# A third staging buffer and biased exponentials in the head stage of a two-block transformer kernel

## The chip, the cores and the metric

The kernel runs on one core of one Trainium2 chip. A core has TensorE (matmuls; PE in the rows, and PEld for its weight loads), VectorE (DVE), ScalarE (ACT), GpSimd (POOL) and SyncE (SP), each with an instruction queue of its own that is worked off in order, and DMA engines. The metric is the time of one execution on the device in microseconds. It covers two different transformer blocks of two layers each over 272 and 256 tokens. Every weight is read from HBM once, everything is computed in float32 precision.

## The reference

Block 1 is a mixer with three branches (retention, hgrn2, differential attention) and a convolutional feed-forward; block 2 has four branches, one of them a gated linear attention of the same form as hgrn2. The change is in how the decay of hgrn2 is applied, of which this is the core:

```python
def hgrn2(q, f_logit, inp, gate, lb, valid):
    log_f = logaddexp(log(max(lbh, LB_FLOOR)), log1p(-lbh) + log_sigmoid(f_logit))
    k = (1.0 - lbh) * sigmoid(-f_logit)
    def step(state, xs):
        qc, kc, vc, lfc = xs
        cb = cumsum(lfc, axis=1)
        dec = where(causal, exp(cb[:, :, None] - cb[:, None, :]), 0.0)
        a = einsum('bqhd,bkhd,bqkhd->bhqk', qc, kc, dec)
        o = einsum('bhqk,bkhe->bqhe', a, vc) + einsum('bqhd,bhde->bqhe', qc * exp(cb), state)
        c_end = cb[:, -1]
        state = exp(c_end)[..., None] * state + einsum('bkhd,bkhe->bhde', kc * exp(c_end[:, None] - cb), vc)
        return state, o
```

There are 8 heads of 128 features, and chunks of 128 tokens (128, 128 and 16).

## The kernel before

**Weights.** All weights come as slabs of eight 128x128 blocks through a ring of six slots. SyncE loads a slab when TensorE has released its slot (slab_used). ScalarE rounds it to ring_hi (L879), VectorE (L1318, in some stretches GpSimd, L2017) subtracts to ring_lo, and only then does TensorE use it. A product is three matmuls a block (hi x hi, lo x hi, hi x lo; L456), so a projection of a 128-feature tile is 24 matmuls and one slab.

**The order.** Each engine's program is written out by hand, in a fixed order; engines wait for each other with counted semaphores (Signal, Banks). PSUM has eight banks that all products take in turn. The head stage is the loop over the eight hgrn2 heads in block 1. TensorE does, for head h: the level products (masked block products at block sizes 64 to 1, "lv"), the products between chunks ("cross"), three projections out of TILES_FILL, the values times the weights, two more projections and the sum of squares. TILES_FILL holds the projections of the other branches, three rotated tiles (rq, rk, dq, dk) and two value tiles (rv, dv) for each head. Behind every projection the tile before it is turned (turn): a rotated tile is multiplied with a rotation matrix, a value tile is transposed (L533).

**Staging.** Before a tile can be turned, ScalarE copies it from PSUM to a buffer of XS (stage; the copy is followed by the drain L941 that signals it). XS has two buffers, so the copy of tile i waits for tile i-2: for a value tile until TensorE has transposed it, for a rotated tile until VectorE has taken it (settle, L1448 to L1453).

**Head h on VectorE:** hg_weights(h) masks and adds the level products (L1368 on); hg_differences(h+1) writes the exponents (L1397 to L1401 and L1352) into Z; then normalise(h-1), and a sequence of slabs and settled tiles; after the first settled tile hg_factors(h+1) multiplies the exponentials with the keys (L1360, L1410 to L1413) and signals z, without which TensorE can't begin the level products of head h+1. ScalarE's exp_levels(h+1) lies between the two, behind the copy of the second tile and ahead of that of the third. Z[:, 3] and Z[:, 8] hold the factors between chunks: the first chunk's keys carried to its end, the second chunk's queries from its start, the first chunk's keys carried to the end of the second (Z[:, 8, 0:P], the product of Z[:, 3, 0:P] and e1, the decay over the whole second chunk), the second chunk's keys carried to its end, and the 16 last queries. HC is the running sum of -log f in each chunk (L1656, eight scans). Block 2 has the same in one piece for its gated linear attention (L1937 to L1942, L1254).

## Time and profile before

| | |
|---|---|
| median of 3 runs | 2497.81 us (2497.37 to 2498.92) |
| the profiled execution | 2496.82 us, span 2495.0 us |
| granted TensorE clock, mean | 0.982 |
| TensorE busy | 2354.8 us, 94% |
| VectorE busy | 1807.5 us, 72% |
| ScalarE busy | 1308.6 us, 52% |
| chain that ended last, share of the span | TensorE 61%, VectorE 22% and its queue 5%, ScalarE 4% |
| head stage, first layer | about 125 to 293 us |
| head stage, second layer | about 883 to 1052 us |

Over the whole span TensorE is the fullest engine, but a share of the span is a mean over stages with different limits. For a change inside a stage one reads that stage: which engine stands, until when, and what it was released by. In the timeline a row gives the start, the duration and, in brackets, the idle time just before it with its releaser; merged rows give their count.

### The profile page before, as it was taken

The page shows a single profiled execution, that of the slowest core. Times are in us where ns is not written, and L with a number is a line of the kernel's source. Part 1 is how long each engine was busy: PE and PEld are TensorE (multiplying, and loading weights), DVE is VectorE, ACT ScalarE, POOL GpSimd, SP SyncE. Part 2 cuts the span into 40 slices and gives each one's busy share as a digit, 9 for nine tenths or more (in the row PEclk, how much of TensorE's full clock was granted, in tenths as well). Part 3 has the DMA queues.
Part 4 walks back from the last instruction along what each step waited for, and adds up shares of the span by engine and source line. Part 5 has one row for each costly group of instructions (what it writes and reads, how often), then busy time and mean ns, then how long its engine had stood idle before and what let it go on. Part 6 is the DMA issues. An engine that isn't in the chain of part 4 may idle for free.

```text
span 2495.0 us, 51424 instructions
## 1 busy us (share of the span) xinstructions
PE 2354.8 (94%) x19438; PEld 2260.7 (91%) x19438; DVE 1807.5 (72%) x3521; ACT 1308.6 (52%) x2192; POOL 387.1 (16%) x492
## 2 busy tenths in 40 slices
PE   7999999998999999999998997989999988998998
PEld 6998898898999998899898997978999988888998
DVE  6689857777875689867777875887766558776764
ACT  5655456755544645556755545545443455455443
POOL 0000003626920000002727910000000000000000
PEclk9999999999999999999999998999999999999999
DMA  6433343344554433343344553433545544344553
GB/s 213 161 112 110 111 144 119 119 161 142 173 177 156 166 119 111 105 157 121 118 164 150 181 183 127 148 123 119 169 163 184 186 139 136 124 136 159 179 181 132
DMA packets 100436, 366.67 MB, mean 147 GB/s; under 512 B 11632, under 2 KB 12144, under 8 KB 99824
## 3 DMA queue, kind: packets, MB, share of 16 engines
q1 hardware_dynamic: 100208, 363.53, 43.5%
q8 instruction: 155, 2.54, 0.4%
q14 instruction: 73, 0.60, 0.1%
HBM read 362.44 MB, written 1.05 MB: 146 GB/s over the span
## 4 chain that ended last, share of the span: by engine, by line
PE 61%; DVE 22%; DVEq 5%; ACT 4%; issue 4%; ACTq 1%; DMA 1%; SPq 0%
PE psum L456 61%; DVE ring_lo L1318 5%; ACT arena L866 2%; DVE arena L1360 1%; DVE arena L1352 1%; DVE arena_r L1306 1%; DMA ring<-w 1%; ACT ring_hi L879 1%; DVE arena_r L1304 1%; DVE arena L1540 1%; PE psum L533 1%; DVEq L1804 1%; DVEq L1298 1%; DVE arena L1537 1%; DVE arena L1368 1%
## 5 line engine op out<-in xcount | busy, mean ns | idle before, releaser
L456 PE MATMUL psum<-hn_hi,ring_hi 128*128 128x272 f32 (+2 forms) x3936 | 1161.2, 296 | 47.5 <-ACT hn_hi L866 20.5
L456 PE MATMUL psum<-hn_hi,ring_lo 128*128 128x272 f32 (+2 forms) x3936 | 1132.5, 289 | 0.0
L456 PE MATMUL psum<-hn_lo,ring_hi 128*128 128x272 f32 (+2 forms) x3936 | 1096.2, 286 | 0.0
L1318 DVE TENSOR_TENSOR ring_lo<-ring,ring_hi 128x1024 fp32r<-128x1024 f32 x562 | 688.8, 1234 | 232.9 <-ACT ring_hi L879 191.0
L456 PEld LDWEIGHTS psum<-hn_hi,ring_hi 128*128 128x128 f32 x3936 | 760.1, 193 | 75.1 <-issue 50.3
L879 ACT ACTIVATE ring_hi<-ring 128x1024 fp32r<-128x1024 f32 x684 | 713.7, 1055 | 215.2 <-DMA ring<-w 185.0
L456 PEld LDWEIGHTS psum<-hn_hi,ring_lo 128*128 128x128 f32 x3936 | 760.8, 193 | 0.0
L456 PEld LDWEIGHTS psum<-hn_lo,ring_hi 128*128 128x128 f32 x3936 | 738.7, 191 | 1.6
L866 ACT ACTIVATE arena<-psum 128x272 f32<-128x272 f32 (+8 forms) x736 | 257.3, 367 | 652.0 <-PE psum L456 533.3
L456 PE MATMUL psum<-arena_r,ring_hi 128*128 128x256 f32 (+2 forms) x2996 | 552.6, 285 | 11.3 <-DVE arena L1854 6.4
L2017 POOL TENSOR_TENSOR ring_lo<-ring,ring_hi 128x256 fp32r<-128x256 f32 x488 | 386.9, 829 | 1060.3 <-ACT ring_hi L879 1060.2
L456 PEld LDWEIGHTS psum<-arena_r,ring_hi 128*128 128x128 f32 x2996 | 464.0, 189 | 15.0 <-DVE arena L1854 6.8
L456 PE MATMUL psum<-arena_r,ring_lo 128*128 128x256 f32 (+2 forms) x1498 | 424.1, 283 | 0.0
L456 PEld LDWEIGHTS psum<-arena_r,ring_lo 128*128 128x128 f32 x1498 | 282.6, 189 | 0.0
L456 PE MATMUL psum<-arena 128*64 128x64 f32 (+12 forms) x2464 | 195.3, 265 | 12.8 <-ACTq L1166 11.6
L456 PEld LDWEIGHTS psum<-arena 128*64 128x64 f32 (+6 forms) x2464 | 149.6, 153 | 58.0 <-issue 19.3
L866 ACT ACTIVATE arena<-arena 128x272 f32<-128x272 f32 (+9 forms) x151 | 87.7, 602 | 96.2 <-DVEq L1298 91.3
L1306 DVE TENSOR_TENSOR arena_r<-arena,arena_r 128x256 fp32r<-128x256 f32 (+2 forms) x150 | 81.4, 543 | 12.6 <-issue 1.7
L866 ACT ACTIVATE arena<-arena,small 128x128 f32<-128x128 f32 (+1 forms) x128 | 59.3, 464 | 55.4 <-DVEq L1298 53.2
L866 ACT ACTIVATE arena<-psum,par_sb 128x272 f32<-128x272 f32 (+1 forms) x88 | 49.6, 566 | 55.9 <-PE psum L456 55.7
L533 PE MATMUL psum<-cst,arena 128*128 128x128 f32 (+4 forms) x292 | 50.1, 273 | 27.6 <-ACTq L941 21.0
L456 PE MATMUL psum<-arena,cst 128*128 128x272 f32 (+2 forms) x232 | 71.1, 403 | 4.4 <-ACTq L1266 3.8
(159 smaller groups left out, 1433.0 us busy)
## 6 DMA issues: line engine op xcount, KB each, us to landing
ring<-w SPq DMA_DIRECT2D x684, 512.0 KB, 3.3
cst<-consts SPq DMA_DIRECT2D x1, 1960.0 KB, 14.0
x_sb<-x_meta SPq DMA_DIRECT2D x1, 1088.0 KB, 4.9
out<-x_sb SPq DMA_DIRECT2D x1, 1024.0 KB, 3.9
arena<-lam SPq DMA_DIRECT2D x1, 256.0 KB, 4.2
par_sb<-par SPq DMA_DIRECT2D x1, 193.0 KB, 4.8
pos_sb<-positions SPq DMA_DIRECT2D x1, 128.0 KB, 6.3
cst<-consts SPq DMA_DIRECT2D x1, 65.5 KB, 4.7
```

The costliest lines, as they stand in the source:

```text
L456: i = nc.tensor.matmul(out_, lhsT=lhsT, rhs=rhs, start=first, stop=last)
L533: t = nc.tensor.transpose(ps[rows, cols], src, ident[0:src.shape[0], 0:src.shape[0]])
L866: i = nc.scalar.activation(out_, in_, func, **kw)
L879: nc.scalar.activation(ring_hi[:, slot], ring[:, slot], ACT.Copy).then_inc(slab_hi[k % RING], 1)
L1298: i = V.drain()
L1304: V.tensor_copy(hi, src)
L1306: return V.tensor_tensor(lo, src, hi.bitcast(F32), ALU.subtract)
L1318: V.tensor_tensor(ring_lo[:, slot], ring[:, slot], ring_hi[:, slot].bitcast(F32), ALU.subtract)\
L1352: V.tensor_tensor(zq[:, z, 0:n].rearrange("p (b t s) -> p b t s", t=2, s=s), paired(C, s, n // (2 * s), step + s), paired(C, s, n // (2 * ...
L1360: V.tensor_tensor(d, d, paired(k, s, n // (2 * s), step + s), ALU.mult)
L1368: V.tensor_tensor(Lt[:, :, :], ps[:, 0:7 * HALF].rearrange("p (a b) -> p a b", b=HALF), lvl[:, :, :], ALU.mult)
L2017: i = nc.gpsimd.tensor_tensor(ring_lo[:, part], ring[:, part], ring_hi[:, part].bitcast(F32), ALU.subtract)
```

## The change

Three things are changed. XS gets a third buffer, so the copy of a staged tile waits for the tile three places before it (the arena grows by one tile of 272 columns). In hg_differences four VectorE subtractions go; the exponents of the factors between chunks are formed by ScalarE's exponential itself, with the running sum as its input and a bias from memory (the negated sum at a chunk's end from PC, or two_sb, the sum of the two chunks' ends, which VectorE makes once behind the scans). So exp_levels has seven activations in place of three, hg_factors loses its last product (with e1) and its drain while the product before it is 256 columns wide instead of 128, and e1 with its exponential and signal goes. In block 2 two subtractions go in the same way, and one exponential of 2048 columns becomes four.

```diff
--- before.py
+++ after.py
@@ -108,7 +108,7 @@
 
 ROUND = 12582912.0
 TWO_PI = [6.28125, 0.0019350051879882812, 3.0199157663446432e-07]
-ARENA = 27736
+ARENA = 27736 + T1
 N_PARAMS = 7
 
 
@@ -306,7 +306,7 @@
         Z, z_end = view(a, 9, T1)
         Y1, _ = view(a, KT, T1)
         a = z_end
-        XS, a = view(a, 2, T1)
+        XS, a = view(a, 3, T1)
         SG, a = view(a, 2, T1)
         S0, a = view(a, T1)
         S1, a = view(a, P + N_META)
@@ -315,7 +315,7 @@
         LT, _ = view(a, 7, HALF)
         SQ, a = view(a, 2, T1)
         TMP, a = view(a, 2, T1)
-        e1_sb, a = view(a, KT)
+        two_sb, a = view(a, KT)
         YS = split_view(0, KT, T1), split_view(KT * T1, KT, T1)
         assert a <= ARENA, a
         c0 = 7 * KT * T1
@@ -413,7 +413,7 @@
             return par2_sb[:, at:at + 1]
 
         STAGED = [k for k in TILES_HG + TILES_FILL if k[0] in VALUES or k[0] in ROT]
-        s1_slot = {k: i % 2 for i, k in enumerate(STAGED)}
+        s1_slot = {k: i % 3 for i, k in enumerate(STAGED)}
 
 
         slab_loaded = [sem(f"slab_loaded{i}") for i in range(RING)]
@@ -431,7 +431,7 @@
             return {n: Signal(sem(section + "_" + n), known.setdefault((section, n), {})) for n in names.split()}
 
         s0 = signals("start", "act dve sq rs total")
-        s1 = signals("one", "sq total rs sqh hn hnlo yb staged taken valued sig_f f_in lnf cum e1 normal crossed sg gated zdiff zexp z att sqo normed "
+        s1 = signals("one", "sq total rs sqh hn hnlo yb staged taken valued sig_f f_in lnf normal crossed sg gated zdiff zexp z att sqo normed "
                      "sco expd w tr y sigm conv ff x")
         s2 = signals("two", "sq total rs normal hn hnlo evac cqn ckn krn qm km oc sg gated gz gez gl gcum zdiff zexp z att sqo normed "
                      "sc expd w tr o relu used y sigm sigf ff x os gls yb")
@@ -934,9 +934,9 @@
                     op(SG[:, h % 2, t0():], ps[:, t0():], ACT.Sigmoid, s1["sg"].done(key))
                 else:
                     i = STAGED.index(key)
-                    if i >= 2:
-                        two = STAGED[i - 2]
-                        act.wait_ge(*(b1.full(two + ("turned",)) if two[0] in VALUES else s1["taken"].upto(two)))
+                    if i >= 3:
+                        old = STAGED[i - 3]
+                        act.wait_ge(*(b1.full(old + ("turned",)) if old[0] in VALUES else s1["taken"].upto(old)))
                     op(XS[:, s1_slot[key], :], ps, ACT.Copy, b1.free(key))
                     nc.scalar.drain().then_inc(*s1["staged"].done(key))
                 feed(b1, key)
@@ -963,9 +963,14 @@
 
             def exp_levels(h):
                 act.wait_ge(*s1["zdiff"].upto(h))
-                op(Z[:, 0:4, 0:2 * P], Z[:, 0:4, 0:2 * P], ACT.Exp)
+                C = HC[:, h, :]
+                op(Z[:, 0:3, 0:2 * P], Z[:, 0:3, 0:2 * P], ACT.Exp)
                 op(Z[:, 4:8, :], Z[:, 4:8, :], ACT.Exp)
-                op(Z[:, 8, P:T1], Z[:, 8, P:T1], ACT.Exp)
+                op(Z[:, 3, 0:P], C[:, 0:P], ACT.Exp, bias=PC[:, P - 1:P])
+                op(Z[:, 3, P:2 * P], C[:, P:2 * P], ACT.Exp, scale=-1.0)
+                op(Z[:, 8, 0:P], C[:, 0:P], ACT.Exp, bias=two_sb[:, h:h + 1])
+                op(Z[:, 8, P:2 * P], C[:, P:2 * P], ACT.Exp, bias=PC[:, 2 * P - 1:2 * P])
+                op(Z[:, 8, 2 * P:T1], C[:, 2 * P:T1], ACT.Exp, scale=-1.0)
                 nc.scalar.drain().then_inc(*s1["zexp"].done(h))
 
             def cross_weights(h):
@@ -1066,9 +1071,6 @@
                         act.wait_ge(*s1["f_in"].upto())
                         log_exp_table()
                         op(HC[:, :, :], HC[:, :, :], ACT.Ln, s1["lnf"].done())
-                    if key == ("hi", 5):
-                        act.wait_ge(*s1["cum"].upto())
-                        op(e1_sb[:, :], HC[:, :, 2 * P - 1], ACT.Exp, s1["e1"].done(), scale=-1.0)
                     if key == ("hi", 7):
                         exp_levels(0)
                 fill = list(TILES_FILL)
@@ -1251,7 +1253,10 @@
                     merge_sigmoid2(1, 2 * h + 1)
                     if h == 1:
                         act.wait_ge(*s2["zdiff"].upto())
-                        op(Z2[:, :, :], Z2[:, :, :], ACT.Exp)
+                        op(Z2[:, 0:3, :], Z2[:, 0:3, :], ACT.Exp)
+                        op(Z2[:, 4:8, :], Z2[:, 4:8, :], ACT.Exp)
+                        op(Z2[:, 3, 0:P], GC[:, 0:P], ACT.Exp, bias=PC[:, P - 1:P])
+                        op(Z2[:, 3, P:T2], GC[:, P:T2], ACT.Exp, scale=-1.0)
                         nc.scalar.drain().then_inc(*s2["zexp"].done())
                 for g in range(GLA_HEADS):
                     if g % 2 == 0:
@@ -1395,10 +1400,6 @@
                     dve.wait_ge(*b1.full(("cross", h - 1)))
                 C = HC[:, h, :]
                 V.tensor_scalar(PC[:, :], C, -1.0, None, ALU.mult)
-                V.tensor_scalar(Z[:, 3, 0:P], C[:, 0:P], C[:, P - 1:P], None, ALU.subtract)
-                V.tensor_scalar(Z[:, 3, P:2 * P], C[:, P:2 * P], -1.0, None, ALU.mult)
-                V.tensor_scalar(Z[:, 8, P:2 * P], C[:, P:2 * P], C[:, 2 * P - 1:2 * P], None, ALU.subtract)
-                V.tensor_scalar(Z[:, 8, 2 * P:T1], C[:, 2 * P:T1], -1.0, None, ALU.mult)
                 V.drain()
                 level_differences(C, PC.offset - C.offset, Z, LV, T1)
                 fence(s1["zdiff"].done(h))
@@ -1407,10 +1408,8 @@
                 dve.wait_ge(*s1["zexp"].upto(h))
                 q, k = HQ[:, h, :], HK[:, h, :]
                 level_factors(Z, [(P, 3)] + LV, T1, k, KT * T1)
-                V.tensor_tensor(Z[:, 8, P:2 * P], Z[:, 8, P:2 * P], k[:, P:2 * P], ALU.mult)
+                V.tensor_tensor(Z[:, 8, 0:2 * P], Z[:, 8, 0:2 * P], k[:, 0:2 * P], ALU.mult)
                 V.tensor_tensor(Z[:, 8, 2 * P:T1], Z[:, 8, 2 * P:T1], q[:, 2 * P:T1], ALU.mult)
-                V.drain()
-                V.tensor_scalar(Z[:, 8, 0:P], Z[:, 3, 0:P], e1_sb[:, h:h + 1], None, ALU.mult)
                 fence(s1["z"].done(h))
 
             def hg_weights(h):
@@ -1654,11 +1653,11 @@
                         dve.wait_ge(*s1["lnf"].upto())
                         for h in range(HG_HEADS):
                             V.tensor_tensor_scan(HC[:, h, :], restart[:, :], HC[:, h, :], 0.0, ALU.mult, ALU.subtract)
-                        fence(s1["cum"].done())
+                        V.drain()
+                        V.scalar_tensor_tensor(two_sb[:, :], HC[:, :, P - 1], -1.0, HC[:, :, 2 * P - 1], ALU.mult, ALU.subtract)
                     if key == ("hi", 5):
                         hg_differences(0)
                     if key == ("hg", 0):
-                        dve.wait_ge(*s1["e1"].upto())
                         hg_factors(0)
                 fill, before = list(TILES_FILL), None
                 for w0 in (S0, S1):
@@ -1935,8 +1934,6 @@
                         V.tensor_tensor_scan(GC[:, :], restart[:, 0:T2], GC[:, :], 0.0, ALU.mult, ALU.subtract)
                         V.drain()
                         V.tensor_scalar(PC[:, 0:T2], GC[:, :], -1.0, None, ALU.mult)
-                        V.tensor_scalar(Z2[:, 3, 0:P], GC[:, 0:P], GC[:, P - 1:P], None, ALU.subtract)
-                        V.tensor_scalar(Z2[:, 3, P:T2], GC[:, P:T2], -1.0, None, ALU.mult)
                         V.drain()
                         level_differences(GC[:, :], PC.offset - GC.offset, Z2, LV, T2)
                         fence(s2["zdiff"].done())
```

## Rows read from the trace of the kernel before

**Rows 1.** Table by stretch: us, busy time (count) of each engine, clock, DMA share, GB/s.
```profile
125.00:293.00 168.00, 157.66 (x1467) 148.85 (x1461) 150.38 (x376) 83.35 (x153) 0.00 (x0) 0.97 0.33 111
...
293.00:340.00 47.00, 46.49 (x409) 45.39 (x410) 32.48 (x56) 25.76 (x45) 0.00 (x0) 1.00 0.40 138
```

**Rows 2.** What TensorE waited for: us in total, times, longest us.
```profile
PE psum L533 <- ACTq L941: 21.0, 12, 2.5
```

**Rows 3.** Timeline, TensorE: start, us, line, operation, tiles, count [wait, releaser].
```profile
144.50 0.49 PE L533 MATMUL psum<-cst,arena 128*128 128x128 f32 x3
...
145.38 0.80 PE L456 MATMUL psum<-arena 128*64 128x64 f32 x20
...
169.31 0.90 PE L533 MATMUL psum<-cst,arena 128*128 128x128 f32 x3 [2.52 <-ACTq L941]
...
171.05 3.81 PE L456 MATMUL psum<-arena 128*64 128x64 f32 x76
...
293.51 0.55 PE L533 MATMUL psum<-cst,arena 128*128 128x128 f32 x3 [1.54 <-ACTq L941]
...
294.45 3.20 PE L456 MATMUL psum<-arena 128*64 128x64 f32 x76
...
1051.67 0.51 PE L456 MATMUL psum<-arena 128*64 128x64 f32 x10
```

**Rows 4.** Timeline, ScalarE, head 2 of the first layer.
```profile
157.61 2.27 ACT L866 ACTIVATE arena<-arena 128x1024 f32<-128x1024 f32 x3 [0.95 <-DVEq L1298]
...
168.83 0.40 ACT L866 ACTIVATE arena<-psum 128x272 f32<-128x272 f32 x1 [4.11 <-DVEq L1298]
```

**Rows 5.** Timeline, VectorE, head 2 of the first layer.
```profile
153.99 0.29 DVE L1397 TENSOR_SCALAR arena<-arena 128x272 f32<-128x272 f32 x1
...
154.97 2.58 DVE L1352 TENSOR_TENSOR arena<-arena 128x256 f32<-128x256 f32 x7
...
162.56 2.91 DVE L1360 TENSOR_TENSOR arena<-arena 128x256 f32<-128x256 f32 x8
...
165.39 0.29 DVE L1410 TENSOR_TENSOR arena<-arena 128x128 f32<-128x128 f32 x1
...
165.84 0.29 DVE L1413 TENSOR_SCALAR arena<-arena 128x128 f32<-128x128 f32 x1
...
166.24 1.23 DVE L1318 TENSOR_TENSOR ring_lo<-ring,ring_hi 128x1024 fp32r<-128x1024 f32 x1
```

**Rows 6.** VectorE's waits for the level products, first and second layer's head stage.
```profile
DVE arena L1368 <- PE psum L456: 0.5, 2, 0.2
...
DVE arena L1368 <- PE psum L456: 0.7, 2, 0.3
```

**Rows 7.** Timeline, VectorE: slab behind hg_factors of heads 1 and 7, both layers.
```profile
141.35 1.23 DVE L1318 TENSOR_TENSOR ring_lo<-ring,ring_hi 128x1024 fp32r<-128x1024 f32 x1
...
290.44 1.23 DVE L1318 TENSOR_TENSOR ring_lo<-ring,ring_hi 128x1024 fp32r<-128x1024 f32 x1
...
899.18 1.23 DVE L1318 TENSOR_TENSOR ring_lo<-ring,ring_hi 128x1024 fp32r<-128x1024 f32 x1
...
1047.66 1.23 DVE L1318 TENSOR_TENSOR ring_lo<-ring,ring_hi 128x1024 fp32r<-128x1024 f32 x1
```

**Rows 8.** Groups by form: out<-in, shapes, count | busy us, mean ns | idle before.
```profile
L866 ACT ACTIVATE arena<-arena,small 128x128 f32<-128x128 f32 x48 | 18.9, 395 | 45.2 <-DVEq L1298 45.2
...
L1360 DVE TENSOR_TENSOR arena<-arena 128x256 f32<-128x256 f32 x80 | 28.6, 423 | 2.6 <-issue 0.9
```

**Rows 9.** Timeline, ScalarE and VectorE, exponentials and factors of head 1.
```profile
135.03 2.27 ACT L866 ACTIVATE arena<-arena 128x1024 f32<-128x1024 f32 x3 [0.43 <-DVEq L1298]
...
137.66 2.91 DVE L1360 TENSOR_TENSOR arena<-arena 128x256 f32<-128x256 f32 x8
```

**Rows 10.** Timeline, TensorE behind the scans.
```profile
88.89 0.36 PE L456 MATMUL psum<-hn_hi,ring_hi 128*128 128x272 f32 x1 [1.62 <-DVE ring_lo L1318]
```

**Rows 11.** Timeline, TensorE in block 2, first layer, before values2.
```profile
1647.92 1.28 PE L456 MATMUL psum<-arena 128*64 128x256 f32 x6 [2.41 <-ACTq L1166]
```

## The prediction

> **What bounds the kernel now.** I read the table by stretch first. In the head stage of block 1's first layer (125 to 293 us) VectorE has 150.4 us of instructions in 168 us and TensorE 157.7 us; in the next 47 us TensorE is full and VectorE has 14.5 us to spare [rows 1]. Both are near full in the head stage, so the table alone doesn't say which one paces it. TensorE's list of waits does: 12 times, 21.0 us in total, the first transpose of a staged tile waits for L941, the drain behind ScalarE's copy into XS [rows 2]. All twelve lie in the two layers' head stages (six in each). I followed one back. TensorE stands 2.52 us until 169.31 [rows 3]. ScalarE's copy for it began at 168.83, after 4.11 us of waiting for VectorE [rows 4]: with two XS buffers the copy of a value tile waits until the tile two places before it has been taken by settle, and VectorE reaches that only after hg_factors and another slab of low halves [rows 5]. VectorE itself hardly waits: 0.5 us in the first layer's stage, 0.7 us in the second's, each time for the level products at L1368 [rows 6]. So VectorE paces the stage with about 24.9 us a head, and the two-buffer rule adds a lag: TensorE begins the level products of a head some 4 us after z of that head is ready. For the last head z is ready where the slab at 290.44 starts, and the products start at 294.45; in the second layer 1047.66 and 1051.67 [rows 3, 7].
>
> **What TensorE needs for a head.** Levels of head 1 begin at 145.38, levels of head 2 at 171.05, 25.67 us later. Of this 2.52 us is the wait. After this wait the clock was low: from the transposes to the levels took 1.74 us where 0.88 us is normal. 25.67 - 2.52 - 0.86 leaves 22.3 us [rows 3]; I take 22.2. The levels that follow at the low clock took 3.81 us, at the full clock 3.20 [rows 3]. A low clock behind one wait costs 0.86 + 0.61 = 1.47 us.
>
> **The change, VectorE's share.** In hg_differences, L1397 begins at 153.99 and the first level difference at 154.97, 0.98 us for five instructions. With L1397 alone it is its 0.29 us and 0.08 for the drain: 0.61 us less. In hg_factors the last product with its drain lasts from 165.84 to 166.24, 0.40 us, and goes; L1410 becomes 256 columns wide where it had 128, 423 ns in place of 0.29 us, 0.13 more: 0.27 us less [rows 5, 8]. Together **0.88 us a head**.
>
> **ScalarE's share.** Three exponentials of 2.27 us become seven [rows 4]. The first loses 256 columns (0.21 us), the 144-column one goes (at least 0.21), and five short ones come. A 128-column one with a bias from memory is 395 ns in the list by form [rows 8]; that also accumulates, so it is a ceiling. Without any overlap the seven take 3.8 us; with each short one starting some 0.1 us before the last has ended, and the two without bias and the 16-column one shorter, 3.1 us. I take 3.1. What hides them: zdiff ends at 154.97 + 2.58 = 157.55 and hg_factors begins at 162.56, 5.0 us in which VectorE normalises, makes a slab and settles a tile [rows 5]. So 1.9 us of cover are left, and even 3.8 us fits. The exception is head 1, where nothing is normalised: zdiff ends at 135.03, hg_factors starts at 137.66 [rows 9]. ScalarE is free from 134.60 (0.43 us before), so its exponentials end at 137.7, and VectorE, ready at 137.05, waits 0.7 us. There only 0.18 of 0.88 us is won. Behind the longer exponentials, ScalarE's queue holds the copy of the third rotated tile. Counted back from z: zdiff is 8.4 us before it, the copy is in place 4.8 us before, and TensorE needs 4.5 us from there to the levels (rotation, one projection, transposes, sum of squares). It arrives just about with z.
>
> Here a rule speaks against the change. The Trainium skill, "ScalarE: Activation LUTs", Rules for kernel authors, says to put additions on VectorE and not on ScalarE. By that rule the four subtractions would stay, and 0.61 us a head with them; the trace speaks for moving them, since ScalarE has half of the stage idle.
>
> **The third buffer.** The value tile's copy now waits for the tile three places before it. That one is settled before hg_factors, 3.9 us before z, and TensorE wants it 0.9 us before z at the earliest. The stall goes. What is late next is z itself: TensorE waits for it about 1.7 us a head (23.9 against 22.2), partly before the third tile's rotation. VectorE doesn't get later for that, because hg_weights comes 6.4 us after z and the levels take 3.2 to 3.8 us.
>
> **The sum.** z of head 1 is ready at 141.35, so then at 141.17. Six heads take 290.44 - 141.35 = 149.09 us; less 6 x 0.88 and less the 0.5 us of waits on TensorE, which now leads, 143.31: z of head 7 at 284.5. TensorE's own pace would have it at head 7 at 145.38 + 6 x 22.2 = 278.6, so z decides. Levels of head 7 begin at 284.6 and not 294.45: **9.9 us**. Second layer: z of head 1 at 899.18, then 899.0; 148.48 - 5.28 - 0.7 = 142.5; z of head 7 at 1041.5, levels at 1041.6 and not 1051.67: **10.1 us** [rows 3, 6, 7]. Behind the stage VectorE is some 3 us further behind TensorE than now; the 14.5 us that it has free by 340 us [rows 1] take that up, so the gain stays.
>
> **The other edits.** Behind the scans come a drain and an 8-column operation. TensorE waits 1.62 us there for the next slab of low halves [rows 10], so it costs time in full: a small VectorE operation, from nothing to 0.2 us, I take 0.1, twice: **+0.2**. Dropping the exponential of e1 frees ScalarE before projections that TensorE does without a wait: nothing. In block 2 two of the four subtractions' kind go from a chain (subtractions, level differences, mask of the next head, its exponential, the turned weights) that ends in a wait of TensorE, 2.41 us [rows 11]: 0.3 us each layer, between nothing and 0.6, so **-0.6**. The split exponential there (0.4 us more) is followed by ScalarE waits: nothing.
>
> Total 9.9 + 10.1 + 0.6 - 0.2 = 20.4 us. The profiled execution took 2496.8 us with a span of 2495.0; it would be 2476.4 with a span of 2474.6. The median of the runs, 2497.8, becomes **2477.4 us**. A measurement of this kernel can tell about 0.2%, 5 us, from no change.
>
> **Rivals.**
> *Only VectorE's work counts.* The lag stays at 4 us, because the copies in ScalarE's queue wait for something else: the third tile behind the longer exponentials (if these take 5 us rather than 3.1) or the next value tile. Then only 0.18 + 5.28 us a layer is won, 10.9 and with the rest 11.3: 2486.5 us. For it: that queue is strictly in order and my margin at z is a few tenths. Against: even 3.8 us leaves the levels late by under 1 us. 14%.
>
> *The change does not do its work*, or the clock eats it: TensorE still waits 1.7 us a head, in two pieces (at the rotation and at z). The clock fell behind the wait of 2.52 us and stayed behind that of 1.54 us [rows 3]; the ten others divide in the same way. Were it to fall at both pieces in each head, TensorE would need 22.2 + 2 x 1.47 = 25.1 us a head and set the pace from head 2 on: levels of head 7 at 145.38 + 22.2 + 5 x 25.1 = 293.1, 1.4 us a layer: 2494.6 us, no change that can be told. With the case that two buffers weren't the reason at all, 9%.
>
> *Slower.* The same place, a longer fall: if the low clock also covers the projection behind the rotation wait. Of a head's 22.2 us some 4.1 are transposes, sum and levels (0.88 + 3.20, [rows 3]); the five projections share 18.1, at most 3.6 us each, and at 1.2 in place of 2.4 GHz up to 3.6 us more. With 1.47 for the levels a head takes 27.3 us, and head 7 begins at 145.38 + 22.2 + 5 x 27.3 = 304.1, 9.6 us later than now; both layers and the rest give 2516.6 us. It decides from (294.45 - 167.6) / 5 = 25.4 us a head, 3.2 us of clock loss in each. Against: the trace shows 1.47 us at most behind a wait, and shorter waits come now. 5%.
>
> The Trainium skill, "TensorE: Matmul & The Clock Gate", Part 1, says that the gate follows how busy the array has lately been and is free-running, so the same waits may or may not meet it. The trace bears that out so far: of the twelve waits half were followed by the low clock.
>
> **Chances and range.** Forecast 72%, rivals 14, 9 and 5%. Within the forecast: the exponentials of head 1 up to 0.7 us longer per layer, the clock low at the last levels (1.47 us per layer), the block 2 term and the scan term put it at 2482 at most; 0.88 us a head may be 0.2 off, 2.8 us over 14 heads, which puts the other end at 2474. The range takes in the first rival: 2474 to 2487. Faster 0.86, the same 0.09, slower 0.05.
>
> **What would show it.** L1398 to L1401 and L1413 gone and the first level difference 0.37 us after the negation. Seven exponentials of together 3.1 us behind each zdiff. No wait of the transposes for L941, or waits of a few tenths; new TensorE waits at the third rotation and at the first level product. Levels of head 7 at 284.6 in the first layer, and in the second at 1031.8 (some 10 us from each layer). VectorE without waits except 0.7 us before hg_factors of head 1. If VectorE has waits for zexp in every head, my price of the exponentials is wrong; if z comes as computed but the levels 4 us later, the third buffer's part is.

## The result and the profile after

| | before | changed | ratio, 95% interval |
|---|---|---|---|
| first comparison | 2498.36 us (4 runs) | 2473.2 us (2471.47 to 2475.71, 4 runs) | 0.9898 [0.9881, 0.9916] |
| the changed kernel once more | 2496.39 us (9 runs) | 2475.6 us (2473.62 to 2476.95, 5 runs) | 0.9909 [0.9896, 0.9923] |

The change makes the kernel about 1% faster. The forecast was 2477.4 us with a range from 2474; as a ratio 2477.4 / 2497.81 = 0.9918. The first median lies 0.8 us under the range, the second inside it. The first interval reaches on both sides of the range's lower end: 0.9881 and 0.9916 of 2498.36 us are 2468.6 and 2477.4 us.

The profiled execution took 2471.47 us with a span of 2469.7, where before took 2496.82 and 2495.0. Its list of TensorE's waits (us in total, times, longest), against [rows 2]:

```profile
PE psum L456 <- DVEq L1303: 29.5, 13, 10.0
PE psum L456 <- ACT hn_hi L866: 20.2, 8, 4.9
PE psum L456 <- DVE ring_lo L1323: 17.3, 18, 3.0
PE psum L456 <- DVE arena L1449: 9.0, 18, 0.9
PE psum L456 <- ACTq L1168: 7.9, 6, 1.7
```

The transposes' 21.0 us behind L941 are gone. New are 18 waits of half a microsecond each for L1449, VectorE's read of a rotated tile in PSUM: the next product needs that bank. The head stages by stretch (us, busy time and count of each engine, clock, DMA share, GB/s), from the first level product of head 0 to the first projection behind head 7, first and second layer. The kernel before:

```profile
123.64:297.49 173.85, 163.00 (x1586) 153.71 (x1586) 155.26 (x386) 87.83 (x160) 0.00 (x0) 0.97 0.33 110
881.49:1054.72 173.23, 163.03 (x1587) 153.83 (x1586) 154.95 (x386) 87.84 (x160) 0.00 (x0) 0.97 0.33 110
```

The changed kernel:

```profile
125.01:290.09 165.08, 159.92 (x1587) 151.07 (x1586) 147.33 (x347) 92.64 (x188) 0.00 (x0) 1.00 0.34 116
873.80:1038.13 164.33, 159.82 (x1587) 151.08 (x1586) 147.04 (x347) 92.62 (x188) 0.00 (x0) 1.00 0.34 117
```

They are 8.8 and 8.9 us shorter, VectorE is busy for 7.9 us less in each, and the granted clock rose from 0.97 to 1.00. Now the rows that the last part of the prediction asked for, on the timelines of the changed kernel (start, duration, line, tiles, count, wait). VectorE, head 1, then head 2, then head 7:

```profile
138.94 2.91 DVE L1365 TENSOR_TENSOR arena<-arena 128x256 f32<-128x256 f32 x8 [0.62 <-ACTq L974]
...
142.39 1.23 DVE L1323 TENSOR_TENSOR ring_lo<-ring,ring_hi 128x1024 fp32r<-128x1024 f32 x1
...
155.06 0.29 DVE L1402 TENSOR_SCALAR arena<-arena 128x272 f32<-128x272 f32 x1
155.42 2.58 DVE L1357 TENSOR_TENSOR arena<-arena 128x256 f32<-128x256 f32 x7
...
285.51 1.22 DVE L1323 TENSOR_TENSOR ring_lo<-ring,ring_hi 128x1024 fp32r<-128x1024 f32 x1
```

ScalarE's seven exponentials of heads 1 and 2:

```profile
135.87 3.01 ACT L866 ACTIVATE arena<-arena 128x768 f32<-128x768 f32 x7
...
158.07 3.03 ACT L866 ACTIVATE arena<-arena 128x768 f32<-128x768 f32 x7
```

TensorE: levels of head 7, the bank wait inside them, the projection behind them, and the levels of head 7 in the second layer:

```profile
285.87 0.28 PE L456 MATMUL psum<-arena 128*64 128x64 f32 x2
...
287.50 0.28 PE L456 MATMUL psum<-arena 128*64 128x64 f32 x2 [0.48 <-DVE arena L1449]
...
290.09 0.40 PE L456 MATMUL psum<-hn_hi,ring_hi 128*128 128x272 f32 x1 [0.33 <-DVE arena L1449]
...
1033.68 0.28 PE L456 MATMUL psum<-arena 128*64 128x64 f32 x2
```

The difference follows the negation by 0.36 us (0.37 was forecast), the exponentials take 3.01 and 3.03 us (3.1), head 1 waits 0.62 us (0.7). From the slab behind z of head 1 to that of head 7 are 285.51 - 142.39 = 143.12 us (143.31), and the levels of head 7 start 0.36 us after z, where they started 4 us after it [rows 3, 7]. From levels of head 0 to levels of head 7 are 160.86 us where 170.81 were: 9.95 us less (9.9); in the second layer 159.88 against 170.18: 10.3 less (10.1). On the clock of the trace the levels of head 7 come at 285.87 and 1033.68, not at 284.6 and 1031.8: both have in them the 1.28 us lost ahead of head 0 of the first layer (below).

TensorE isn't held up in every head. The levels of the heads 1, 2 and 3 start at 146.75, 168.82 and 190.90, in steps of 22.07 us, its own pace (22.2 in the forecast), because z of head 1 is 4.4 us ahead of it. From head 4 on the steps are 23.0 to 24.1 us, and VectorE sets the pace.

So up to the levels of head 7 the stage came as computed. The two profiled spans are 25.3 us apart, and the two stages explain 17.7. The stretches, cut at the same matmul in each kernel (TensorE's starts; us; the first counts from the first matmul, and the stretch between the blocks, 8.66 us and then 8.50 three times, is left out):

| stretch | before | before, again | changed | changed, again |
|---|---|---|---|---|
| start to head 0, layer 1 | 113.68 | 113.43 | 114.96 | 113.69 |
| head stage 1 | 173.86 | 174.11 | 165.08 | 165.05 |
| rest of block 1, layer 1 | 478.82 | 478.85 | 478.13 | 478.08 |
| projections, layer 2 | 105.18 | 105.16 | 105.59 | 105.50 |
| head stage 2 | 173.23 | 174.07 | 164.32 | 164.37 |
| rest of block 1, layer 2 | 462.96 | 462.79 | 463.55 | 463.47 |
| block 2, layer 1 | 280.38 | 280.06 | 274.93 | 277.76 |
| its feed-forward | 197.96 | 198.83 | 197.99 | 198.03 |
| block 2, layer 2 | 280.21 | 281.98 | 276.46 | 280.22 |
| its feed-forward | 200.33 | 201.68 | 200.39 | 200.62 |

In block 2 the first pair of traces is 9.2 us apart, where I had forecast 0.6.

The first line hides a loss that isn't the change's. The same 30 matmuls of the first projections, far ahead of any edited instruction, in the kernel before and in the changed one:

```profile
34.27:38.14 3.87, 3.87 (x30) 3.87 (x31) 2.65 (x3) 2.13 (x6) 0.00 (x0) 1.00 0.68 252
34.08:39.47 5.39, 5.39 (x31) 5.39 (x31) 3.44 (x3) 2.22 (x6) 0.00 (x0) 0.68 0.47 164
```

In the first trace of the changed kernel the clock was low there, and this cost 1.5 us; in its second trace it was not. From there to head 0 are 85.50 us before and 85.54 or 85.55 in both traces of the changed kernel.

### The profile page after: what moved, and what is told of

It reads as the page before. It is cut to its first block, busy times and chain, and to the rows that moved or that the text cites. A ratio compares the mean times of both kernels' runs of the same rounds, so it can differ in the third digit from the quotient of the medians.

```text
span 2469.7 us, 51390 instructions
## 1 busy us (share of the span) xinstructions
PE 2349.1 (95%) x19438; PEld 2255.9 (91%) x19438; DVE 1796.9 (73%) x3439; ACT 1319.4 (53%) x2260; POOL 387.5 (16%) x492
## 4 chain that ended last, share of the span: by engine, by line
PE 61%; DVE 23%; DVEq 5%; ACT 5%; issue 4%; ACTq 2%; DMA 1%; SPq 0%
PE psum L456 60%; DVE ring_lo L1323 6%; ACT arena L866 2%; DVE arena L1365 2%; ACT ring_hi L879 1%; DVE arena_r L1311 1%; DVE arena L1357 1%; DMA ring<-w 1%; DVE arena_r L1309 1%; DVE arena L1539 1%; DVEq L1303 1%; DVEq L1803 1%; DVE arena L1536 1%; PE psum L533 1%; DVE arena L1452 1%
## 5 line engine op out<-in xcount | busy, mean ns | idle before, releaser
L456 PEld LDWEIGHTS psum<-arena 128*64 128x64 f32 (+6 forms) x2464 | 146.0, 147 | 60.3 <-issue 16.2
L866 ACT ACTIVATE arena<-arena 128x128 f32<-128x128 f32 (+6 forms) x219 | 100.3, 502 | 123.5 <-DVEq L1303 119.0
L1311 DVE TENSOR_TENSOR arena_r<-arena,arena_r 128x256 fp32r<-128x256 f32 (+2 forms) x150 | 81.9, 546 | 11.5 <-issue 0.4
L1309 DVE CAST arena_r<-arena 128x256 fp32r<-128x256 f32 (+2 forms) x150 | 61.4, 410 | 12.7 <-issue 1.3
```

The lines of the kernel that those rows point to most:

```text
L456: i = nc.tensor.matmul(out_, lhsT=lhsT, rhs=rhs, start=first, stop=last)
L866: i = nc.scalar.activation(out_, in_, func, **kw)
L1309: V.tensor_copy(hi, src)
L1311: return V.tensor_tensor(lo, src, hi.bitcast(F32), ALU.subtract)
```

## Experiments

### Taking the change apart

Theory A says that block 2 gained by its own edit, theory B that it is where stretches at the lower clock fall.

The head stage's part alone; block 2 keeps its code of before:

```diff
-                        op(Z2[:, 0:3, :], Z2[:, 0:3, :], ACT.Exp)
-                        op(Z2[:, 4:8, :], Z2[:, 4:8, :], ACT.Exp)
-                        op(Z2[:, 3, 0:P], GC[:, 0:P], ACT.Exp, bias=PC[:, P - 1:P])
-                        op(Z2[:, 3, P:T2], GC[:, P:T2], ACT.Exp, scale=-1.0)
+                        op(Z2[:, :, :], Z2[:, :, :], ACT.Exp)
```

(with its two subtractions back on VectorE).

> The changed kernel with block 2 as it was before. In the profile of the changed kernel the two head stages give 8.8 and 8.9 us and block 2's first stages (from the norm to the output product) 5.5 and 3.8 us, where 0.6 us was forecast. Theory A, it is block 2's own edit: this kernel is 16 to 18 us faster than before (about 2481.5), and its block 2 stages last 280 us as before. Theory B, it is where the low-clock stretches of TensorE fall in block 2, whatever shifts them: this kernel is within 2 us of the changed one (about 2474), with block 2 stages anywhere from 275 to 281 us in its one profile.

The kernel before with block 2's edit alone, so that diff the other way round:

> The kernel before with block 2's edit alone (two subtractions less on VectorE, four exponentials in place of one on ScalarE, in each layer). Theory A: 7 to 9 us faster than before, about 2490, with block 2's first stages at 275 to 277 us. Theory B: 0.6 us as forecast, at most 2 us either way, about 2497.8.

The kernel before with the third buffer alone (the wait goes three tiles back and the arena grows by a tile, as in the change):

```diff
-        XS, a = view(a, 2, T1)
+        XS, a = view(a, 3, T1)
-        s1_slot = {k: i % 2 for i, k in enumerate(STAGED)}
+        s1_slot = {k: i % 3 for i, k in enumerate(STAGED)}
```

> The kernel before with the third XS buffer alone. Forecast: VectorE still needs 24.9 us a head, but the lag of 4 us between z of head 7 and its level products goes: 4 us a layer, less 1.2 us for the wait on a PSUM bank that the changed kernel shows inside the level products: 2.8 to 4 us a layer, 6 to 8 us in all, about 2491; no transposes waiting for the staging copy. Rival (only VectorE's work counts): under 2 us, about 2497.

The exponentials and VectorE's shorter work in the head stage alone, two buffers, block 2 as before:

> The changed kernel's exponentials and shorter VectorE work in block 1 with two XS buffers and block 2 as before. Forecast: 0.88 us less a head on VectorE, 5.5 us a layer, 10 to 11.5 us in all, about 2487.5; the lag of 4 us and the 12 waits of the transposes for the staging copy stay. Rival (the clock's falls decide): the waits get shorter than the longest ones that are followed by the low clock, and it gains up to 5 us more, about 2483.

| | median us (runs) | ratio, interval | head stages | block 2, two layers |
|---|---|---|---|---|
| before, beside them | 2498.44 (23) | | 173.86, 173.23 | 280.38, 280.21 |
| head stage only | 2477.57 (5) | 0.9917 [0.9904, 0.9930] | 165.10, 164.36 | 277.88, 280.00 |
| block 2 only | 2495.66 (11) | 0.9992 [0.9984, 1.0001] | 173.20, 172.54 | 277.33, 279.59 |
| third buffer only | 2490.05 (12) | 0.9975 [0.9966, 0.9983] | 170.57, 169.70 | 277.52, 281.33 |
| exponentials only | 2482.20 (5) | 0.9947 [0.9933, 0.9961] | 167.69, 166.91 | 277.59, 278.88 |

The head stage's part alone gives 20.9 us; its terms in the forecast were 19.8 with the scans. The third buffer alone shortens a stage by 3.3 and 3.5 us, VectorE's and ScalarE's part alone by 6.2 and 6.3; together they would be 9.5 and 9.9, and both at once give 8.8 and 8.9. Each part alone already lifts the granted clock of both stages from 0.97 to 1.00, so what the clock gives back is in both numbers. Without the third buffer the transposes keep twelve waits,

```profile
PE psum L533 <- ACTq L941: 17.6, 12, 1.8
```

and with it alone the bank waits appear, and the waits for VectorE's queue, 29.4 us and 13 in the kernel before, grow by ten, five in each head stage, where VectorE is still at its old pace:

```profile
PE psum L456 <- DVEq L1298: 37.2, 23, 10.0
...
PE psum L456 <- DVE arena L1450: 12.1, 21, 0.9
```

Against what was expected: the third buffer alone gave 8.4 us in the medians (6 to 8) and 3.3 and 3.5 in the stages (2.8 to 4), so the rival's 2 us is refuted. The exponentials alone gave 16.2 us and not 10 to 11.5, near the rival's 2483: their waits are no longer than 1.8 us, and the clock didn't fall in the head stages (1.00). But of the 16.2 only 12.5 lie in the head stages, where 5.5 a layer were forecast; the other 3.7 lie outside them. For the head stage's part alone, theory A's 16 to 18 us don't fit 20.9; it lies 2.0 or 4.4 us above the two medians of the changed kernel, so theory B's 2 us is neither met nor refuted. Block 2's edit alone gave 2.8 us, where theory A wanted 7 to 9 and theory B 2 at most; its interval takes in no change at all.

Against theory A: three kernels whose block 2 is that of before have it 2.5 to 2.9 us shorter in the first layer. The edit itself can be read where it works, over the 71 matmuls ahead of the product that waits for ScalarE, with the wait: this stretch comes twice in each trace. With the old code (six traces of this study) it is 11.62 or 11.63 us eleven times and 12.16 once; with the new code (eight traces) 11.28 to 11.30 us twelve times and 11.47 or 11.48 four times. The edit is worth 0.33 us a layer; the forecast said 0.3.

### The same programs again

> The changed kernel once more, nothing edited. Theory A (block 2 is shorter by its own edit): block 2 is again about 9 us shorter than in the trace of the kernel before. Theory B (it is where the stretches at a lower granted clock fall, in steps of about 1.5 us, and that wanders from execution to execution): the runs spread over 4 us or more, single parts of block 2 differ from the first profile of the changed kernel by 1.4 to 1.6 us, and the median lies at 2472 to 2478 us; the two head stages are again 8.8 us shorter each within 0.4.

> The kernel before once more, nothing edited. Theory B (stretches at a lower granted clock wander through block 2 and the feed-forward parts with unchanged code): the head stages, which wait in every head, repeat within 0.3 us (173.9 and 173.2 us), while one of the two long parts of block 2 differs by 1.4 us or more from the first trace of this kernel (280.4 and 280.2 us). Rival: the trace of a kernel repeats in every part within 0.3 us, and a difference of 1.4 us between two kernels is due to their code.

The changed kernel: 2475.6 us; its trace is in the table above. Head stages 165.05 and 164.37; block 2 of the first layer 2.83 us longer than in the first trace, that of the second 3.76 us longer, with not one instruction changed. The kernel before: 2498.92 us (2494.18 to 2503.66, 10 runs), ratio 1.0003 [0.9991, 1.0016]; block 2's second part 1.77 us longer than in its first trace, its first within 0.4. What I had not expected is that its second head stage differs by 0.84 us. So 6.6 of the 9.2 us of block 2 are gone again in a second execution of the same program: these, at least, are not the edit's.

A delay between the blocks while TensorE stands, on the kernel before:

```diff
             enter("middle")
+            for _ in range(3):
+                V.tensor_copy(pad_sb[:, :], fin_sb[:, 0:1].to_broadcast([P, 256]))
+                V.drain()
```

(pad_sb is a new tensor that nothing else uses.)

> The kernel before, with three copies of 256 columns on VectorE between the blocks, each waited for, while TensorE stands still: about 1 us, and nothing else of the program changed. Theory B (block 2's length depends on where its stretches at a lower clock fall, which a shift of 1 us can move): the part between the blocks is 1 us longer, and the parts of block 2, whose code is that of before, differ by multiples of 1.4 to 1.6 us or not at all. Rival: the time is longer by 1 us and no part but the one with the copies changes.

Measured 2497.65 us (10 runs), ratio 1.0000 [0.9987, 1.0012]. The stretch between the blocks grew from 8.50 us (the second trace of before) to 9.60, and block 2's second part was 278.39 us where 281.98 and 280.21 were: 1.1 us of pure delay can't be found in the time, whose interval is 3 us wide on either side. The differences are not clean multiples of 1.5 us, as I had expected. The rivals, that a trace repeats within 0.3 us everywhere and that only the delayed part changes, are refuted, and theory B holds for most of block 2's 9.2 us.

Here is one such step, in block 2 of the first layer: the stretch before the product that waits for ScalarE, the product, and the projection behind it. The kernel before (the clock is the third number from the end):

```profile
1636.30:1647.92 11.62, 9.21 (x71) 8.63 (x71) 10.01 (x26) 5.20 (x10) 0.00 (x0) 1.00 0.27 97
1647.92:1650.60 2.68, 1.72 (x8) 0.99 (x8) 2.37 (x4) 2.48 (x3) 0.00 (x0) 0.96 0.00 0
1650.60:1656.15 5.55, 5.55 (x34) 5.55 (x35) 3.77 (x7) 2.60 (x7) 0.00 (x0) 0.71 0.26 96
```

The changed kernel:

```profile
1618.43:1629.90 11.47, 10.81 (x72) 9.70 (x72) 9.76 (x24) 5.20 (x10) 0.00 (x0) 0.85 0.29 99
1629.90:1632.57 2.67, 1.72 (x8) 0.98 (x9) 2.35 (x4) 2.48 (x4) 0.00 (x0) 1.00 0.00 0
1632.57:1636.71 4.14, 4.14 (x34) 4.14 (x35) 3.77 (x7) 2.97 (x9) 0.00 (x0) 1.00 0.35 127
```

The count behind each engine's busy time is in brackets. Before, the low clock (0.71) lies behind the wait, and the projection takes 5.55 us. In the changed kernel it lies ahead of the wait (0.85), in time that TensorE would have stood anyway: the wait is 0.66 us where it was 2.41 [rows 11], the product starts 0.18 us later than without the low clock, and the projection takes 4.14. What the stretch takes without the low clock is seen in the last version below (both later edits at once), whose block 2 is the changed one:

```profile
1613.34:1624.63 11.29, 9.20 (x71) 8.62 (x72) 9.68 (x24) 5.20 (x10) 0.00 (x0) 1.00 0.29 98
```

There the wait is 2.09 us, so of the fall from 2.41 to 0.66 us only 0.3 are the edit's; the rest of the wait is filled by the slower matmuls. The same loss is paid in full in one trace and nearly hidden in the other. On the timeline before, the starts of the matmuls show which level it was, 0.22 us for 256 columns, 1.2 GHz; in the changed kernel 0.12 us, 2.4 GHz:

```profile
1651.41 0.41 PE L456 MATMUL psum<-hn_hi,ring_hi 128*128 128x256 f32 x1
1651.63 0.41 PE L456 MATMUL psum<-hn_lo,ring_hi 128*128 128x256 f32 x1
```

```profile
1633.27 0.28 PE L456 MATMUL psum<-hn_hi,ring_lo 128*128 128x256 f32 x1
1633.39 0.28 PE L456 MATMUL psum<-hn_hi,ring_hi 128*128 128x256 f32 x1
```

All traces together: in the six of kernels with the old block 2, the projection behind this wait (two in each) was lengthened by the low clock in 6 of 12 cases, by 1.4 to 2.4 us; in the eight with the new code in 1 of 16. Block 2 with its feed-forward parts takes 955.4 to 962.6 us in the former (mean 958.1), 949.8 to 959.4 in the latter (mean 955.2): 2.9 us apart, with spreads of 7 and 10 us. That a shorter wait there also makes the low clock rarer would fit; these counts suggest it and don't settle it.

### What paces the head stage

TensorE's new bank waits, undone by order: VectorE reads the tile first.

```diff
                         if before is not None:
-                            low(b1, before, 4)
                             settle(before)
+                            low(b1, before, 4)
```

> The changed kernel, with VectorE reading a staged tile's rotated PSUM bank before it makes the next slab of low halves, not behind it. Theory (the 18 waits of TensorE for VectorE's read of a rotated tile, 9.0 us in all, 0.5 us ahead of each level product, cost about 0.6 us a layer that the prediction did not have): those waits fall to under 3 us in all, and the head stage shortens by 0.3 to 0.6 us a layer, so 0.5 to 1.2 us in all. Rival (VectorE's total work paces the heads, and the order inside a head changes nothing): the waits move to the slabs' low halves, the head stages stay within 0.2 us, the time within 0.5 us of the changed kernel's.

Measured 2474.47 us, 1.1 less than the changed kernel beside it (2475.6), ratios 0.9908 [0.9894, 0.9921] and 0.9909: not told apart. But in the trace the head stages are 164.35 and 163.57 us, 0.7 and 0.8 shorter, and the waits for L1449 are gone from the head stage; 3.3 us for L941 and 1.8 us for low halves stand in their place (first layer). The rival is refuted; the stages gained a little more than the 0.3 to 0.6 us of the theory. Where the gain is: from the levels of head 7 to the first projection behind them are 3.05 us in both layers, as in the kernel before, where the changed kernel takes 4.22 and 4.45:

```profile
286.30 3.19 PE L456 MATMUL psum<-arena 128*64 128x64 f32 x76
289.35 0.39 PE L456 MATMUL psum<-hn_hi,ring_hi 128*128 128x272 f32 x1
```

Inside the heads the new order costs: the levels of head 7 come 0.4 and 0.6 us later behind those of head 0.

ScalarE's chain lengthened:

```diff
                 op(Z[:, 8, 2 * P:T1], C[:, 2 * P:T1], ACT.Exp, scale=-1.0)
+                for u in range(12):
+                    op(pad_sb[:, 35 * u:35 * u + 35], C[:, 0:35], ACT.Copy)
```

> The changed kernel, with twelve copies of 35 columns (about 0.22 us each by rows of such widths, 2.6 us) on ScalarE behind the exponentials of every head of block 1, ahead of the signal to VectorE. Theory (the seven exponentials of 3.0 us lie under 5.0 us of VectorE's other work, in all heads but the first): the first 2.0 us added are hidden, so heads 1 to 7 lengthen by about 0.6 us each or less and head 0 by 2.6 us: 4 to 8 us a layer, 8 to 15 us in all, about 2483 us. Rival (ScalarE's chain is not covered, each us on it lengthens the head): 2.6 us for each of 16 heads, 42 us in all, 2514 us. Second rival (cover is larger than 5.0 us): only head 0's 2.6 us a layer show, 5 us in all.

Measured 2484.91 us (2483.01 to 2489.11), 9.3 us more. The group of the copies and VectorE's wait in head 1:

```profile
L867 ACT ACTIVATE pad_sb<-arena 128x35 f32<-128x35 f32 x192 | 24.9, 217 | 0.0
```

```profile
142.20 1.10 DVE L1368 TENSOR_TENSOR arena<-arena 128x256 f32<-128x256 f32 x3 [2.37 <-ACTq L977]
```

Each copy lasts 217 ns but they overlap: 24.9 us for 192 are 0.13 us each, 1.6 us a head and not 2.6. Head 1's wait grew by 1.75 us, and the head stages by 1.7 and 1.5; ahead of head 0 the stretches are 1.5 and 1.9 us longer than in the first trace of the changed kernel. That makes 6.7 us; where the rest of the 9.3 lies the traces don't tell from the scatter of block 2. In no other head of either layer does VectorE wait for the exponentials: the cover of 5.0 us holds 3.0 + 1.6. The first rival is refuted. Theory and second rival are not told apart, since 4.6 us don't reach the end of a cover of 5.0.

One slab of low halves a head moved from VectorE to GpSimd:

```diff
+POOL_SLABS |= {layer * SLABS1 + 36 + 5 * h for layer in range(DEPTH) for h in range(7)}
```

> The changed kernel, with one slab of low halves in each of the heads 0 to 6 of both layers' first stage made by GpSimd in place of VectorE. Theory (behind the third buffer VectorE's work of 23.9 us a head paces the heads, and TensorE's own need is 22.2): each of seven heads shortens by the slab's 1.2 us, 6 to 8 us a layer in the head stage, 12 to 17 us in all: about 2459 us. Rival 1 (ScalarE's chain behind the differences, or the staging of tiles, paces them): under 3 us in all. Rival 2 (GpSimd takes 3.3 us for a slab, so TensorE waits for its low halves): the head stages are longer, about 2 us for each of 14 slabs where nothing covers it, up to 28 us in all, 2500 us.

Measured 2481.1 us, 5.5 us more; the head stages are 167.13 and 166.75. TensorE never waits for GpSimd's low halves there, so neither the theory nor its second rival, as I had put them, is right; the first rival's 3 us is exceeded too. GpSimd's slab, and VectorE beside it:

```profile
200.26 2.93 POOL L2015 TENSOR_TENSOR ring_lo<-ring,ring_hi 128x256 fp32r<-128x256 f32 x4 [20.93 <-ACT ring_hi L880]
```

```profile
200.53 0.67 DVE L1379 TENSOR_TENSOR arena<-arena 128x128 f32<-128x128 f32 x1
201.28 1.30 DVE L1382 TENSOR_TENSOR arena<-arena 64x64 f32<-64x64 f32 x2
```

The same work in the changed kernel:

```profile
199.71 0.29 DVE L1378 TENSOR_TENSOR arena<-arena 128x128 f32<-128x128 f32 x1
200.08 0.45 DVE L1381 TENSOR_TENSOR arena<-arena 64x64 f32<-64x64 f32 x2
```

While GpSimd works, VectorE's small operations take 1.97 us in place of 0.74: the 1.2 us that the slab was to save are lost again. It is so in the whole stage: the five additions of 128x128 that lie under GpSimd's slab take 0.67 us, the nine others 0.29, and although VectorE has seven slabs less, it is busy for 148.93 us where it was 147.33. And the loss lies ahead of the differences: in the later heads of the first layer the way from the level weights to the negation takes 7.57 us in place of 6.34, the way from there to the factors 6.49 in place of 7.61. So ScalarE's exponentials come later in a head, and the third tile's copy in its queue with them. TensorE's wait in the first layer's head stage:

```profile
PE psum L457 <- ACTq L942: 6.6, 6, 1.4
```

A relief that doesn't slow VectorE's other work: ScalarE negates the sums ahead of need.

```diff
+            def negated_sums(h):
+                op(PC[:, :], HC[:, h, :], ACT.Copy, scale=-1.0)
+                nc.scalar.drain().then_inc(*s1["neg"].done(h))
 ...
-                V.tensor_scalar(PC[:, :], C, -1.0, None, ALU.mult)
-                V.drain()
+                if h > 0:
+                    dve.wait_ge(*s1["neg"].upto(h))
+                else:
+                    V.tensor_scalar(PC[:, :], C, -1.0, None, ALU.mult)
+                    V.drain()
```

(ScalarE makes the sums of head 1 before the heads begin, those of head h+2 behind the last tile of head h.)

> The changed kernel, with the negated sums of heads 1 to 7 made by ScalarE ahead of need in place of VectorE (0.29 us and the wait behind it, 0.37 us a head in VectorE's chain). Theory (VectorE's work and its chain from one head's weights to the next's factors pace the heads): the head stage shortens by 0.37 us for each of seven heads, 2.2 to 2.6 us a layer, 4.4 to 5.2 us in all: about 2470.5 us. Rival 1 (TensorE or ScalarE paces the heads by now): under 1 us in all. Rival 2 (the 0.4 us added on ScalarE holds up its staging): longer, up to 0.4 us a head, 6 us in all.

Measured 2472.66 us (2468.77 to 2474.64), ratio 0.9895 [0.9876, 0.9913]. Its head stages by stretch:

```profile
124.99:287.69 162.70, 158.72 (x1586) 150.77 (x1585) 145.22 (x340) 95.49 (x195) 0.00 (x0) 1.00 0.35 118
872.78:1034.68 161.90, 158.74 (x1586) 150.80 (x1586) 144.91 (x340) 95.53 (x195) 0.00 (x0) 1.00 0.35 119
```

2.4 us less in each stage, seven times 0.34 where 0.37 was taken off VectorE: it comes off the stage nearly one for one, as the theory has it. Rivals 1 and 2 are refuted for the stage. The time itself, 0.5 and 2.9 us under the changed kernel's two medians, doesn't tell. The two edits at once:

> The changed kernel with both edits: ScalarE negates the sums, and VectorE reads a rotated tile's PSUM bank ahead of the next slab of low halves. Theory (VectorE paces, and each bank wait adds to it): 4.4 to 5.2 us of the negation and 1.4 us of the order, 6 us in all: about 2469.5 us, head stages of 162 and 161.3 us. Rival (one limit takes over from the other): no more than the larger of the two alone, head stages of 162.6 and 161.9 us.

Measured 2473.7 us (2469.83 to 2475.08), ratio 0.9893 [0.9875, 0.9912]; head stages 161.96 and 161.53 us, the first as the sum of the two, the second 0.4 us short of it. Both versions have shorter head stages than the changed kernel, by 2.4 and 3.1 us and by 2.4 and 2.8. Their times don't show it: the forecasts were 2470.5 and 2469.5 us, and the intervals overlap with the changed kernel's own (0.9898 and 0.9909). In the traces block 2 took it back (its two parts took 3.5 and 3.0 us more in the first, 4.9 and 4.1 in the second than in the first trace of the changed kernel); for the medians that is only likely.

## Why the prediction was right or wrong

**What bounds the kernel, and the sum for the head stage: right.** VectorE paced the stage and does so still from head 4 on: moving 0.37 us a head off it shortened the stages by 2.4 us each. The two terms, 9.9 and 10.1 us at the levels of head 7, measured 9.95 and 10.3. Their parts were right one by one: the third buffer takes away the lag, the differences lose 0.6 us, seven exponentials cost 3.0 us and are hidden but in head 1. One more place was overlooked, head 0: there ScalarE's copies behind the longer exponentials come later. In the second layer VectorE waits 4.10 us for the first of them where it waited 3.35, its slabs fall behind, and TensorE waits for one, which costs it 0.45 us. First the row before, then two of the changed kernel:

```profile
864.16 0.42 DVE L1458 TENSOR_TENSOR arena<-arena,psum 128x258 f32<-128x258 f32 x1 [3.35 <-ACT arena L866]
```

```profile
856.83 0.42 DVE L1457 TENSOR_TENSOR arena<-arena,psum 128x258 f32<-128x258 f32 x1 [4.10 <-ACT arena L866]
...
862.22 0.36 PE L456 MATMUL psum<-hn_hi,ring_hi 128*128 128x258 f32 x1 [0.28 <-DVE ring_lo L1323]
```

"TensorE waits for it about 1.7 us a head" was wrong as put: only from head 5 on does a head take so much longer (23.8 to 24.1 us against 22.07), and the wait lies inside the levels and behind them, at the banks, not at the rotation or at z. The sum didn't use it.

**"So the gain stays": wrong by 1.2 and 1.4 us in the first pair.** At the projection behind head 7 only 8.8 and 8.9 us are left. I had listed what comes late next (z) and not the PSUM banks: eight banks that all products take in turn stand in the description of the kernel, and with TensorE no longer held by the transposes it asks for a rotated tile's bank before VectorE has read it, behind a slab of 1.2 us. With the other order these 1.2 and 1.4 us are gone, and 0.7 and 0.8 us are left of that after what the order costs inside the heads.

**Block 2's edit was priced right, 0.33 us a layer for 0.3.** The scans cost 0.04 and 0.03 us where 0.1 was in the sum: so much longer are the sixty matmuls around them. The 1.28 us ahead of head 0 in the first pair are the low clock at 34 us.

**The clock, rivals two and three: did not come.** All waits in the new head stage are under 1 us, and the granted clock is 1.00 over the whole of it. The waits of 1.5 and 2.5 us by which I priced the fall of the clock are no longer there; I had split the idle time of a head into two pieces, but kept the price of one piece. And with the exponentials alone, twelve waits of 1.1 to 1.8 us left the clock at 1.00. The rule of the Trainium skill, "TensorE: Matmul & The Clock Gate", Part 1, that the gate is free-running, agrees with the later runs: the same program had block 2 2.8 and 3.8 us apart in two executions, mostly in steps of 1.3 to 1.6. What I had offered for it wasn't evidence: of the twelve waits in the trace before, all six of 2.20 to 2.52 us were met by the low clock and none of the six of 0.80 to 1.54 us, which looks like order. The kernel with block 2's edit alone, with the same head stage, is the evidence: its first layer has four waits of 2.29 to 2.52 us, and the clock fell at two of them.

**The step that failed: the term for block 2, 0.6 us, and a range that let the clock only take time there and nowhere give it back.** The lower end, 2474, took 2.8 us for VectorE's pace and nothing for the clock; for the clock I had only losses, all in the head stages. Block 2 measured 9.2 us in the first pair of traces and 4.1 in the second, of which the edit's own step is 0.66. In the first trace of the changed kernel block 2 with its feed-forward parts is 5.6 us or more under all six traces with the old code, and the first median came out 0.8 us under the range. That is less than the scatter: the four runs behind it went from 2471.47 to 2475.71, and beside the last experiments 21 runs of the kernel before from 2491.36 to 2503.13; this alone wants some 2 us on either side (an estimate from these spreads). By the two kernels that isolate block 2's edit the term would be 2.8 us (block 2 only against before) and 4.4 or 2.0 (head stage only, 2477.57, against the changed kernel's 2473.2 and 2475.6), each no surer than 2 us. How much of it is the edit's doing beyond 0.66 us stays open.

**How near the total came is in part luck.** By the first pair of traces, 25.3 us apart, the sum of 20.4 had 20.0 for the head stages (17.7 came), a loss of 0.2 ahead of them (1.7 came, 1.28 of it the clock at 34 us) and 0.6 for block 2 (9.2 came). The errors have different signs. In the second pair, 24.2 us apart, the same parts are 18.8, 0.6 and 4.1, and 1.9 more came in the feed-forward parts of block 2, whose code is unchanged.

The rule on additions, from the Trainium skill, "ScalarE: Activation LUTs", Rules for kernel authors, which spoke against the change, would have kept 0.6 us a head on VectorE. The measurement decides for the trace: with the exponentials alone the head stages are 6.2 and 6.3 us shorter, and of the 0.88 us a head by which VectorE is relieved 0.61 come from the four subtractions; VectorE paced the stage, and ScalarE had half of it idle. Here the additions ride on the exponentials as their bias, and the seven take ScalarE 0.74 us a head more than the three did (3.01 against 2.27). The negation, moved alone, gave 0.34 us a head.

## What to carry over

Ask which engine has no idle time in the stage, price each instruction taken from it in full, and check by a small relief that the stage follows nearly one for one. See too which engine is ahead at the start of the stage: its lead has to be used up before the other's pace shows. When a buffer is added, go on to the next resource that the freed engine takes in turn, here the PSUM banks, and see who reads them last and behind what. Where other parts of the program lose time to the clock in steps, let the range have room for that on both sides, and judge a change of under 0.2% by the stretch that it touches and not by the time.

## What the runs showed of the hardware

- While GpSimd made a slab (2.93 us), VectorE's small SBUF operations were slowed: 0.29 to 0.67 us for 128x128, 0.45 to 1.30 for two of 64x64. With seven slabs of 1.2 us moved to GpSimd VectorE was busy for 1.6 us more in the stage, not for 8.6 less.
- Short ScalarE activations in a row overlap: twelve copies that last 217 ns each cost 0.13 us each, seven exponentials, three of them with a bias from memory, 3.0 us.
- A stretch at the lower clock cost about 1.4 to 1.5 us where TensorE was the limit (5.55 against 4.14 us, 5.39 against 3.87) and 0.18 us or nothing where it fell ahead of a wait for another engine: clock 0.85 in a stretch of 11.47 or 11.29 us, 11.29 at clock 1.00.
- In the head stages the clock fell at waits of about 2.2 to 2.5 us, not at each of them (two of four in the first layer of the kernel with block 2's edit alone), and at none of the twelve waits of 1.1 to 1.8 us of the kernel with the exponentials alone.
